# A mixer and expert encoder: the first experts' weight splits set ahead of the end of the block table, the place search split between the start and the expert loop, the end sums kept in PSUM

## What is computed

```python
def _hier_moe(h, w_rg, b_rg, w_re, b_re, w_gate, w_up, w_down):
    ...
    g_prob = jax.nn.softmax(g_logits.astype(jnp.float32), axis=-1)
    ...
    gate = jax.nn.softmax(top_val.astype(jnp.float32), axis=-1) * p_group
    ...
    padded = ((counts + MOE_BLOCK - 1) // MOE_BLOCK) * MOE_BLOCK
    pad_end = jnp.cumsum(padded)
    ...
    block_expert = jnp.minimum(jnp.searchsorted(pad_end, block_start, side='right'), N_EXPERTS - 1)
    x_blocks = h[slot_tok].reshape(n_blocks, MOE_BLOCK, d)

    def expert_block(args):
        xb, e = args
        hid = jax.nn.silu(xb @ w_gate[e]) * (xb @ w_up[e])
        return hid @ w_down[e]

    y = lax.map(expert_block, (x_blocks, block_expert)).reshape(n_slots, d)
    return jnp.zeros((n_tok, d), y.dtype).at[slot_tok].add(y * slot_w[:, None])
```

## Time and profile before

| | us |
|---|---|
| median of 3 runs (lowest to highest) | 1419.27 (1417.82 to 1432.27) |
| the profiled execution | 1419.24 |
| its span, first to last instruction | 1417.6 |
| busy TensorE, VectorE, ScalarE, GpSimd | 1316.5, 1094.3, 867.6, 431.7 |

### The profile page before, as it was taken

How to read it: one execution, slowest core, us unless ns; L and a number is a source line. 1 busy time by engine, 2 the same in 40 slices (tenths; PEclk the granted TensorE clock), 3 DMA queues, 4 the chain that set the end, 5 groups by cost and what they waited for, 6 DMA issues and landing times. The chain is left out here.

```text
span 1417.6 us, 25108 instructions
## 1 busy us (share of the span) xinstructions
PE 1316.5 (93%) x8518; PEld 1113.0 (79%) x8518; DVE 1094.3 (77%) x1497; ACT 867.6 (61%) x1168; POOL 431.7 (30%) x479
## 2 busy tenths in 40 slices
PE   4999999978898879999998899999999999999995
PEld 4999778868887878668887688888888888888872
DVE  5895797775778758645667888888888888888857
ACT  7474344565565454552223677777777777777744
POOL 6020089008666737312101111111111111111136
PEclk9999999988999989999998999999999999999997
DMA  9175888411233129812015999999999999999966
GB/s 271 45 227 152 269 246 236 126 41 52 48 105 119 26 107 344 326 28 95 31 45 212 358 402 414 412 413 410 408 415 412 408 412 414 407 410 413 368 225 234
DMA packets 154826, 357.51 MB, mean 252 GB/s; under 512 B 44000, under 2 KB 100604, under 8 KB 127484
## 3 DMA queue, kind: packets, MB, share of 16 engines
q1 hardware_dynamic: 131899, 297.04, 56.0%
q0 software_dynamic: 14976, 40.43, 8.5%
q10 hardware_dynamic: 7872, 19.01, 3.4%
HBM read 287.64 MB, written 68.78 MB: 251 GB/s over the span
## 5 line engine op out<-in xcount | busy, mean ns | idle before, releaser
L2916 PE MATMUL gate_up_mm<-w_hi,gathered_T_hi 128*128 128x512 f32 x528 | 212.2, 402 | 7.8 <-DVE gathered_T_lo L3127 7.7
L2918 PE MATMUL gate_up_mm<-w_hi,gathered_T_lo 128*128 128x512 f32 x528 | 208.2, 394 | 0.0
L2917 PE MATMUL gate_up_mm<-w_lo,gathered_T_hi 128*128 128x512 f32 x528 | 207.8, 394 | 0.0
L3122 DVE TENSOR_TENSOR w_lo<-w_down,w_hi 128x2048 fp32r<-128x2048 f32 x66 | 148.5, 2289 | 58.5 <-ACT w_hi L3036 58.5
L2846 POOL COPY gather_idx<-upto_pair 128x1 int32 (+1 forms) x34 | 14.5, 427 | 510.5 <-PE x_turned L2906 470.6
L3036 ACT ACTIVATE w_hi<-w_up 128x2048 fp32r<-128x2048 f32 x66 | 126.6, 1920 | 50.7 <-PE down_mm L2953 50.0
L3122 DVE TENSOR_TENSOR w_lo<-first_w_gate,w_hi 128x2048 fp32r<-128x2048 f32 x66 | 150.1, 2290 | 7.7 <-ACT w_hi L3036 7.6
L3122 DVE TENSOR_TENSOR w_lo<-w_up,w_hi 128x2048 fp32r<-128x2048 f32 x66 | 150.6, 2287 | 4.0
L3036 ACT ACTIVATE w_hi<-w_down 128x2048 fp32r<-128x2048 f32 x66 | 123.7, 1915 | 45.3 <-issue 22.1
L3036 ACT ACTIVATE w_hi<-first_w_gate 128x2048 fp32r<-128x2048 f32 x66 | 127.0, 1925 | 31.2 <-PE gate_up_mm L2918 30.5
L2916 PEld LDWEIGHTS gate_up_mm<-w_hi,gathered_T_hi 128*128 128x128 f32 x528 | 100.6, 191 | 34.2 <-issue 13.0
(11 more groups left out here) (529 smaller groups left out, 3122.2 us busy)
## 6 DMA issues: line engine op xcount, KB each, us to landing
w_up<-in_expert_w_up SPq DMA_DIRECT2D x66, 1024.0 KB, 8.3
w_down<-in_expert_w_down SPq DMA_DIRECT2D x66, 1024.0 KB, 7.0
first_w_gate<-in_expert_w_gate SPq DMA_DIRECT2D x64, 1024.0 KB, 8.1
expert_rows_dram<-ones SPq DMA_DIRECT2D x32, 512.0 KB, 6.9
expert_rows_dram<-expert_out ACTq DMA_DIRECT2D x32, 512.0 KB, 8.5
x<-s_rows_dram SPq DMA_DIRECT2D x9, 1184.0 KB, 6.3
s_rows<-s_rows_dram SPq DMA_DIRECT2D x7, 1184.0 KB, 6.3
w_raw<-in_w_in SPq DMA_DIRECT2D x12, 512.0 KB, 5.3
```

Source lines behind the costliest of these rows:

```text
L2916: pe.matmul(dst, xT_hi[:, k, :], hi[:, at, cols], start=k == 0, stop=False)
L2917: pe.matmul(dst, xT_hi[:, k, :], lo[:, at, cols], start=False, stop=False)
L2918: mm = pe.matmul(dst, xT_lo[:, k, :], hi[:, at, cols], start=False, stop=k == KT - 1)
L3122: dve.tensor_tensor(lo[:, at, :], flat(j), hi[:, at, :].bitcast(F32), ALU.subtract).then_inc(S["piece_lo"], 1)
```

## The change

The table is built in three parts, and piece 0 of the first expert is split by VectorE before the last of them. ScalarE splits the first weights first and makes its exponentials later. The first gather takes its indices from where they lie. Fewer matmuls of `keep_clock` stand in the start, and 9 new ones ahead of the loop. `places` is cut in four: `gates` stays in the start, `places_in_order`, `places_before_last` and the one-hots (`turned_places`, four in a pass) move to the ends of passes 1 to 6 of VectorE's loop. At the end, the first of the two adds writes to PSUM and the second reads it from there; `old_rows` waits for the second. The diff, cut:

```diff
-            gather(0, 0, 1)
+            pool.indirect_dma_start(out=xg[:, 0, :], out_offset=None, in_=h_dram,
+                                    in_offset=bass.IndirectOffsetOnAxis(ap=rt["slot_tok"][:, 0:1], axis=0)
+                                    ).then_inc(gathered[0], 16)
+            pool.sem_inc(S["turn"], 1)
...
-            keep_clock(12)
-            block_table()
-            keep_clock(8)
+            keep_clock(3)
+            table_starts()
+            keep_clock(2)
+            table_blocks()
+            keep_clock(2)
             pe.wait_ge(gathered[0], 16)
             turn_rows(0)
-            keep_clock(8)
+            keep_clock(6)
...
             turn_rows(1)
+            keep_clock(9)
...
-                    pe.wait_ge(S["add"], 2 * (t - 4) + 1)
+                    pe.wait_ge(S["add"], 2 * (t - 4) + 2)
...
-            act.activation(kept["group"][:], kept["group"][:], ACT.Exp).then_inc(S["gates"], 1)
-            act.wait_ge(S["small"], 1)
-            act.activation(kept["top"][:, 1], kept["top"][:, 1], ACT.Exp).then_inc(S["gates"], 1)
             for j in range(2):
                 split(0, j, 16, None)
             rows_out(0)
             for j in (2, 3):
                 split(0, j, 16, None)
+            act.activation(kept["group"][:], kept["group"][:], ACT.Exp).then_inc(S["gates"], 1)
+            act.wait_ge(S["top"], 1)
+            act.activation(kept["top"][:, 1], kept["top"][:, 1], ACT.Exp).then_inc(S["gates"], 1)
             silu(2)
             act.wait_ge(S["piece_hi"], 4)
             act.sem_inc(S["piece_hi"], 2)
             split(1, 0, 32, 3)
+            rows_out(1)
             split(1, 1, 32, 4)
-            rows_out(1)
...
-            block_table()
-            for j in range(2):
+            table_starts()
+            table_ends()
+            rest(0, 0, 1)
+            table_blocks()
+            rows_rest(0)
+            for j in range(1, 4):
                 rest(0, j, j + 1)
-            rows_rest(0)
-            for j in (2, 3):
-                rest(0, j, j + 1)
-            places()
+            gates()
             dve.wait_ge(S["piece_lo"], 4)
             dve.sem_inc(S["piece_lo"], 2)
             rest(1, 0, 7)
+            rows_rest(1)
             rest(1, 1, 8)
             hidden(0, 4)
-            rows_rest(1)
...
+                with dve.If(i < 7):
+                    with dve.If(i == 1):
+                        places_in_order()
+                    with dve.If(i == 2):
+                        places_before_last()
+                    for part in range(4):
+                        with dve.If(i == part + 3):
+                            turned_places(2 * part)
...
-                dve.scalar_tensor_tensor(out=x1[:, t, :], in0=row_buffer(t, 0), scalar=gate_f[:, 0, t:t + 1],
-                                         in1=sum_ps[t % 4][:].rearrange("p a n -> p (a n)"),
-                                         op0=ALU.mult, op1=ALU.add).then_inc(S["add"], 1)
+                so_far = sum_ps[t % 4][:].rearrange("p a n -> p (a n)")
+                dve.scalar_tensor_tensor(out=so_far, in0=row_buffer(t, 0), scalar=gate_f[:, 0, t:t + 1],
+                                         in1=so_far, op0=ALU.mult, op1=ALU.add).then_inc(S["add"], 1)
...
                 dve.scalar_tensor_tensor(out=x1[:, t, :], in0=row_buffer(t, 1), scalar=gate_f[:, 1, t:t + 1],
-                                         in1=x1[:, t, :], op0=ALU.mult, op1=ALU.add).then_inc(S["add"], 1)
+                                         in1=so_far, op0=ALU.mult, op1=ALU.add).then_inc(S["add"], 1)
```

79 lines of the change are left out of this document (46 added, 33 removed).

## The result

The changed kernel took 1412.61 us (median of 8 runs, 1411.0 to 1418.47), the kernel before in the same comparison 1421.08 us (8 runs, 1417.82 to 1432.27): ratio 0.993, 95% interval 0.9908 to 0.9952. That is 8.5 us faster where 14.2 were forecast, and 1412.6 us lies just above the range. Measured again beside the kernel before, on two other chips, the unaltered changed kernel came to 0.9888 (0.9872 to 0.9905; median 1408.58 us) and 0.9912 (0.9882 to 0.9941; 1409.29 us).

What follows compares the result with a forecast made beforehand. The expert loop runs at TensorE's pace; ahead of it TensorE waits for VectorE, and behind it VectorE loses time. Start 9.2 + end 5.4 - loop 0.4 = 14.2 us off 1419.27: 1405.0 us, range 1400.5 to 1411.

Steps and rivals of the forecast that it cites:

- Start, steps 1 to 9: Ahead of the expert loop: earlier table, gather, splits and moved search work let block 2 start sooner, 9.2 us gained.
- step 9: Start: later-than-needed loads and loop-entry register loads may show; 0.5 us for both off the middle case of 9.7.
- steps 3 and 4: Start: first gather issued about 753.95, landing 4.7 us later; rows turned 759.1 to 760.1; block 0 4.7 us earlier.
- Loop: Expert loop: work moved onto VectorE is covered by its 2.20 us idle per pass; 0.4 us lost, bounds 0 and 6.3.
- End: Sums after the loop: both adds free of GpSimd, VectorE following the last sum directly; 5.4 us gained.
- The PSUM-writing add: End: first add now writes PSUM, shown by no row; taken as 1.26 us like the nearest row, extra cost 0.
- B: Rival: loads or the loop's entry set the start, 5 us of its gain go: 1410 us; chance 0.18.
- C: Rival: the end keeps its stall, the PSUM-writing add being slow or still excluded: 1408 to 1410.5 us; chance 0.08.
- D: Rival: the work moved into the loop is not covered, 6.3 us: 1411 us; chance 0.12.
- E: Rival: VectorE's longer loop body must be fetched again each pass, two fetches giving 1459 us; chance 0.05.

Runs made afterwards that it cites:

- f1: The changed kernel unaltered, run again on chip D: ratio 0.9888 to the kernel before, median 1408.58 us.
- g1: The changed kernel unaltered, run a third time, on chip E: ratio 0.9912 to the kernel before, median 1409.29 us.
- e5: The changed kernel with SyncE issuing a 4-byte transfer behind each of the 16 result-row gathers, chip B: end 46.6 us, no ratio given.
- e4: The changed kernel with the rest of the place search and the 16 one-hots back in the start, out of the loop, chip A: ratio 0.9964.
- e3: The changed kernel with at most four gathers of result rows under way, chip A: ratio 0.9923 to the kernel before.
- e8: The changed kernel with at most eight gathers under way, a limit that never made GpSimd wait, chip B: ratio 0.9941 to the kernel before.
- f4: The changed kernel with the old adds, second run, chip D: ratio 0.9964 to the kernel before, median 1418.82 us.
- e6: The changed kernel with the old adds and at most four gathers under way, chip B: ratio 0.9924 to the kernel before.
- e2: The changed kernel with the old adds (second add with both inputs in SBUF), chip A: ratio 0.9942 to the kernel before.

## Why the prediction was right or wrong, point by point

- **Start, steps 1 to 9: right in sum.** 9.2 us forecast, 8.75 in the changed kernel's profile, 9.6 in f1, 8.6 in g1. The gap is not the 0.5 us that step 9 took off, but steps 3 and 4: the gather is issued 0.7 us into the stage, not at once, and lands 5.2 us later, not 4.7; the rows are turned at the lower clock (1.95 us, not 1.0), which I had only weighed for block 0's matmuls; those run at the higher level from the second on. f1 and e5 have block 0 9.3 to 9.4 us into the stage and not 10.3, so this differs between executions. The parts behind it are as worked out: `gates()` 3.17 us (3.3 forecast), block 1 15.1 us behind block 0 (14.9), block 2 19.0 behind block 1 (19.2).
- **Loop: small, as said, for another reason.** 0.4 us forecast, 0.6 measured in the first pair; over all profiles the loop takes 564.3 to 565.2 us with the old start and 565.5 to 567.5 with the new one. But e4, with none of the moved work in it, needs 566.0: the moved work itself doesn't show, and what the rest is stays open.
- **End: the step that failed.** "Then t = 7: sum at 1399.87, two adds to 1402.6" lets VectorE's adds follow TensorE's sums at once. It put the wait for TensorE's signal at nothing, on the one profile of before, in which t = 0 to 4 do follow within 0.1 us. In the profile after they don't: the signals of t = 1 to 4 come 3.8, 7.4, 4.0 and 0.7 us late, VectorE makes up for it only at 2.65 us per t, and the last add ends 6.0 us behind the last sum instead of 2.7. 2.2 us are left of 5.4. Why the signals are late stays open. On the chips where the signals are in time the step holds, and the gain was put too small, 5.4 for 6.4 us: GpSimd starts its products 15.0 us behind the first sum (f1: 1384.94 against 1369.96), not 18.7 as before, because no old add stretches its issues, so that the norm of t = 6 starts 0.2 us behind the last add.
- **The PSUM-writing add**, which no row of before showed, takes 1.27 to 1.29 us: the value that I took. By the rule of the Trainium skill's "SBUF — State Buffer", section "Who interferes with whom", both adds are free of GpSimd and the norm is not: the trace agrees, 1.28 against 3.23 us.
- **The absolute time.** The forecast started from an execution whose mixers were the shortest of 20 (753.96; the others 756.3 to 764.3). I took one execution's time for the median's, as they agreed to 0.03 us; 3.55 of the 7.5 us by which I was off are that.
- **Rivals.** B (start held by loads or loop entry, 1410): ScalarE waits 2.08 us for `w_up`, but the start gained 8.75 of the 9.2 us. C (end keeps its stall, 1408 to 1410.5) is the nearest to what happened in time and place, but neither of its mechanisms shows: no add is slow. D (work in the loop not covered): the loop takes 0.6 us more, not 6.3. E (the body is fetched again): one instruction packet, as before. A late signal was in none of them.

No version beats the changed kernel everywhere: holding the gathers to four costs 0.5 us at the end on chips D and E, and on chip A its end is 39.5 us (e3) beside 43.2 with the same adds and no limit (e4).

## What to carry over

When a change takes away a stall that you can see, look at what else the stalled instruction waited for, and at what moves into its place: here 6.4 us were there on some chips, and on others 4 of them (in e8 all) went to signals that no row of before had shown late. A theory that forecasts three numbers right can still be wrong about the mechanism; one cheap mark of the disputed moment (a 4-byte transfer on an idle queue) refuted what three edits had seemed to support. And take the base of a forecast from several executions: here the untouched part alone differs by 10 us.

## What the runs showed of the hardware

- TensorE's signals can reach VectorE up to 11 us behind the matmul that sends them, several then 0.1 us apart, while VectorE's to ScalarE come in 0.1 us (e8: add done 1375.45, ScalarE starts 1375.55). Seen in six of the fifteen profiles whose gathers nothing holds back, all six on chips A and B or in the first comparison, and in none on C, D and E; in the five profiles with at most four gathers under way never by more than 0.4 us.
- Sixteen gathers issued 1.24 us apart land in order, 1.27 us apart from the fifth on, 4.3 us behind their issue at first and 6.3 at last (e5).
- An add with both inputs in SBUF stretches GpSimd's issue of a gather from 0.94 to 1.8 or 1.9 us if it has started first (f4, e6; an issue begun near the end of such an add takes 1.03 us, e2), and the other way round GpSimd's products hold it for 8 to 9 us when they run back to back, but only for 0.7 to 0.8 us each when they come one at a time (e2).
